# A PEER layer by dense matmuls over streamed expert tables in place of gathers

## The reference

```python
x = x + gate_m * y
h2 = rms_norm(x, norm_ffn) * (1 + scale_f) + shift_f
# for each token t, head h of 8
q = (h2 @ w_query).reshape(tokens, 8, 2, 128)
s = einsum('thpd,pkd->thpk', q, sub_keys)         # 2 x 128 key scores
s1, i1 = top_k(s[:, :, 0], 16); s2, i2 = top_k(s[:, :, 1], 16)
cand = s1[..., :, None] + s2[..., None, :]        # 256 sums
top_s, top_c = top_k(cand, 16)
e1, e2 = i1 at top_c // 16, i2 at top_c % 16
idx = e1 * 128 + e2                               # one of 16384 experts
g = softmax(top_s)
a = gelu(einsum('thkd,td->thk', expert_down[idx], h2))
out = x + gate_f * einsum('thk,thkd->td', g * a, expert_up[idx])
```

## Time and profile before

| | |
|---|---|
| median of 3 runs | 3375.26 us (3372.39 to 3380.6) |
| span of the profiled execution, first to last instruction | 3373.3 us |
| PE busy | 2396.1 us, 71% |
| DVE busy | 2288.6 us, 68% |
| ACT busy | 1584.8 us, 47% |
| POOL busy | 1313.6 us, 39% |
| DMA moved | 1143.75 MB, mean 339 GB/s |

### The profile page before, as it was taken

The page is one execution under the profiler, slowest core; times in us unless marked ns, Lnnn a source line. Parts: engine busy times, 40 slices in busy tenths (PEclk is TensorE's granted clock), DMA queues, the critical chain, the costliest instruction groups (busy, mean ns, idle before and its releaser), DMA issues.

```text
span 3373.3 us, 39537 instructions
## 1 busy us (share of the span) xinstructions
PE 2396.1 (71%) x13234; PEld 1954.9 (58%) x13234; DVE 2288.6 (68%) x6287; ACT 1584.8 (47%) x2643; POOL 1313.6 (39%) x1166
## 2 busy tenths in 40 slices
PE   5967899957666666766766667666666676666666
PEld 4654577526665555655565556555555566555555
DVE  6873665368987777767777767766777776775554
ACT  3213333215555555545555555555545554555454
POOL 1141600014544444444434444434444444444554
PEclk9989789978887767777777777777777777776666
DMA  6600100249999999999999999999999999999997
GB/s 240 183 13 16 51 1 1 102 176 416 420 421 414 421 408 422 409 421 409 421 401 421 407 421 409 421 408 420 403 421 406 421 408 421 409 421 414 419 421 324
DMA packets 172956, 1143.75 MB, mean 339 GB/s; under 512 B 22384, under 2 KB 23296, under 8 KB 41680
## 3 DMA queue, kind: packets, MB, share of 16 engines
q0 software_dynamic: 148352, 1077.61, 77.4%
q1 hardware_dynamic: 23168, 59.42, 4.9%
q10 hardware_dynamic: 1232, 4.20, 0.3%
HBM read 1131.59 MB, written 8.39 MB: 338 GB/s over the span
## 4 chain that ended last, share of the span: by engine, by line
DMA 42%; DVE 17%; PE 9%; issue 8%; ACT 5%; POOL 1%; POOLq 0%; DVEq 0%; SPq 0%
DMA pair_b<-in_experts_dram,idx_g 24%; DMA pair_a<-in_experts_dram,idx_g 17%; DVE pair_b L1480 4%; PE outs L1267 2%; DVE pair_a L1480 2%; PE outa L1267 2%; ACT pair_b L1348 2%; PE outs L1292 2%; PE outa L1292 2%; ACT pair_a L1348 2%; DMA wq<-in_w_query_dram 1%; DVE top_i L1405 1%; POOL pair_b L1224 1%; DVE top_i L1408 1%; DVE hot L1438 1%
## 5 line engine op out<-in xcount | busy, mean ns | idle before, releaser
L1224 POOL DMA_INDIRECT pair_b<-in_experts_dram,idx_g x612 | 714.1, 1167 | 835.9 <-PE outs L1267 382.4
L1480 DVE SCALAR_TENSOR_TENSOR pair_b<-pair_b,h 128x1024 f32<-128x1024 f32 x612 | 749.0, 1224 | 417.6 <-DMA pair_b<-in_experts_dram,idx_g 410.3
L1348 ACT ACTIVATE pair_b<-pair_b,w 128x1024 f32<-128x1024 f32 x612 | 697.1, 1139 | 306.2 <-DVE w L1474 299.6
L1224 POOL DMA_INDIRECT pair_a<-in_experts_dram,idx_g x412 | 479.8, 1165 | 718.4 <-PE outs L1267 273.6
L1480 DVE SCALAR_TENSOR_TENSOR pair_a<-pair_a,h 128x1024 f32<-128x1024 f32 x412 | 504.2, 1224 | 281.3 <-DMA pair_a<-in_experts_dram,idx_g 275.5
L1267 PE MATMUL outa<-ident,pair_b 128*128 128x128 f32 x2448 | 469.7, 358 | 239.9 <-ACT pair_b L1348 234.4
L1267 PE MATMUL outs<-ident,pair_b 128*128 128x128 f32 x2448 | 441.7, 343 | 246.8 <-ACT pair_b L1348 244.9
L1267 PEld LDWEIGHTS outa<-ident,pair_b 128*128 128x128 f32 x2448 | 384.9, 186 | 320.4 <-ACT pair_b L1348 315.6
L1348 ACT ACTIVATE pair_a<-pair_a,w 128x1024 f32<-128x1024 f32 x412 | 469.2, 1139 | 205.2 <-DVE w L1474 199.0
L1267 PEld LDWEIGHTS outs<-ident,pair_b 128*128 128x128 f32 x2448 | 363.4, 178 | 317.8 <-ACT pair_b L1348 317.6
L1344 ACT ACTIVATE ga<-a 128x1 f32<-128x1 f32 x1024 | 206.9, 202 | 697.9 <-DVE pair_b L1480 395.1
(11 more groups left out here) (343 smaller groups left out, 2508.1 us busy)
## 6 DMA issues: line engine op xcount, KB each, us to landing
wada<-in_w_ada_t_dram SPq DMA_DIRECT2D x48, 512.0 KB, 5.7
pair_b<-in_experts_dram,idx_g POOLq DMA_INDIRECT x612
wq<-in_w_query_dram SPq DMA_DIRECT2D x4, 2048.0 KB, 31.0
pair_a<-in_experts_dram,idx_g POOLq DMA_INDIRECT x412
ht<-in_x_t_dram ACTq DMA_DIRECT2D x4, 1024.0 KB, 16.1
wout<-in_w_out_dram SPq DMA_DIRECT2D x1, 4096.0 KB, 13.7
x<-in_x_dram SPq DMA_DIRECT2D x8, 512.0 KB, 6.5
out_dram<-x SPq DMA_DIRECT2D x8, 512.0 KB, 2.6
```

What stands on the lines that cost most here:

```text
L1224: p.indirect_dma_start(pair[n % R], None, A["experts"], bass.IndirectOffsetOnAxis(ap=idx[:, t % (2 * PH), k:k + 1], axis=0)).then_inc(pair ...
L1348: s_.activation(pair[n % R][:, D:], pair[n % R][:, D:], ACT.Copy, scale=w[:, n % NA:n % NA + 1]).then_inc(scaled, 1)
L1480: v.scalar_tensor_tensor(down, down, 1.0, S.h2[:, n // P, :], ALU.mult, ALU.mult, accum_out=a[:, n % NA:n % NA + 1]).then_inc(dotted, 1)
```

## The change

There are no gathers any more. All 16384 experts are computed for all tokens, and what a token did not pick is masked to zero.

- The tables are laid out anew outside of the launch: `down_units` and `up_units` are 128 units of 512 KB each. A unit is the 128 experts with one second key e2, over all first keys e1. SP streams them through a ring of six (`R = 6`).
- Tokens are four groups of 256, and each group has two passes, one for each half of the units. Phase A of a pass (`dots`) makes, for 64 units, dots of 128 experts with 256 tokens; ACT takes the gelu of two units at a time from PSUM into `dense`, 64 KB a partition. Phase B (`sums`) multiplies `dense` by the up units and accumulates in PSUM for the group. Phases A and B of different passes alternate: A0 A1 B0 A2 B1 A3 B2 and so on to B6 B7.
- The masks: for 8 tokens at a time DVE makes one-hot rows of e1 (`hot1`, 128 wide) and of e2 times the softmax weight (`hot2`, 64 wide) over the 128 picks of a token, PE multiplies the two for each token (`spread_gates`), and DVE multiplies `dense` by the outcome (`mask`). 32 such batches a pass are set between the units of the neighbouring phases, one after every two or three units.
- Queries and scores of all 64 tasks are done before the loop, a tile at a time after the next tile's output projection (`ask`). The scores (128 KB a task) and the transposed h2 go out to DRAM and come back by POOL's and SP's queues. The search is as before, 24 tasks before the loop over passes on DVE and 40 inside it; it keeps e1, e2 and the softmax weight (`picks`) instead of a joint index, and PE turns them (`turn_picks`).
- x2 is held two tiles at a time and spilled to the output in DRAM; the final sum is gated and added row by row (`finish`), with a fourth transposed row for the gate, so that the row transposes are 32 in place of 24.

```diff
-    R, NA = 10, 16
+    GROUP = 2 * P
+    GROUPS = SEQ // GROUP
+    HALF_E = PK // 2
+    PASSES = 2 * GROUPS
+    BT = 8
+    BATCHES = GROUP // BT
+    R = 6
...
+    phases = [("A", 0), ("A", 1)]
+    for p in range(PASSES - 2):
+        phases += [("B", p), ("A", p + 2)]
+    phases += [("B", PASSES - 2), ("B", PASSES - 1)]
...
         def _(sp):
...
+            for n in range(UNITS):
+                kind, p = phases[n // HALF_E]
+                u = n % HALF_E
...
+                if n >= R:
+                    sp.wait_ge(used, n - R + 1)
+                table = A["down_units"] if kind == "A" else A["up_units"]
+                sp.dma_start(ring[:, n % R], table[HALF_E * (p % 2) + u]).then_inc(unit_in[n % R], 16)
...
         def _(pool):
-            for n in range(SLOTS):
...
-                p.indirect_dma_start(pair[n % R], None, A["experts"],
-                                     bass.IndirectOffsetOnAxis(ap=idx[:, t % (2 * PH), k:k + 1], axis=0)).then_inc(pair_in[n % R], 16)
+            for task in range(TASKS):
+                pool.wait_ge(score_kept[task % 4], 16 * (task // 4 + 1))
+                if task >= 2:
+                    pool.wait_ge(s_read, task - 1)
+                pool.dma_start(tsc[:, task % 2], score_dram[task]).then_inc(tsc_in[task % 2], 16)
...
         def _(pe):
...
-            def add_up(n):
...
+            def ask(i):
+                turn(i)
+                for h in range(PH + 1):
+                    if h < PH:
+                        queries(PH * i + h)
+                    if h >= 1:
+                        scores(PH * i + h - 1)
...
+                else:
+                    ask(i - 1)
+            ask(NT - 1)
...
+            def spread_gates(p, b):
+                at = EVENT["gates", p, b]
+                pe.wait_ge(hot_ready, BATCHES * p + b + 1)
+                if at >= 2:
+                    pe.wait_ge(gate_read, at - 1)
+                for j in range(BT):
+                    last = t.matmul((qb, sb)[at % 2][:, j * HALF_E:(j + 1) * HALF_E], hot1[:, b % 2, j, :], hot2[:, b % 2, j, :],
+                                    start=True, stop=True)
+                last.then_inc(spread, 1)
+
+            def dots(n, p, u):
...
+                for k in range(KD):
+                    last = t.matmul(bank[:, (u % 2) * GROUP:(u % 2 + 1) * GROUP], ring[:, n % R, k * P:(k + 1) * P], hg[:, :, k, :],
+                                    start=k == 0, stop=k == KD - 1)
+                last.then_inc(used, 1)
+
+            def sums(n, p, u):
+                q = p // 2
+                if u == 0:
+                    pe.wait_ge(gate_read, EVENT["gates", p, BATCHES - 1] + 1)
...
+                for a in range(2):
+                    for half in range(2):
+                        last = t.matmul(accs[a][:, half * 512:(half + 1) * 512], bufs[p % 2][:, u, a * P:(a + 1) * P],
+                                        ring[:, n % R, half * 512:(half + 1) * 512],
+                                        start=p % 2 == 0 and u == 0, stop=p % 2 == 1 and u == HALF_E - 1)
+                last.then_inc(used, 1)
...
         def _(act):
...
+                    s_.activation(bufs[p % 2][:, 2 * m:2 * m + 2, :].rearrange("p u n -> p (u n)"), (t0, t1)[pair % 2][:],
+                                  ACT.Gelu_apprx_tanh).then_inc(gelu_done, 1)
+                    if p == 0 and m == 11:
+                        softened(1)
...
         def _(dve):
...
+            def make_hot(p, b):
...
+                own.mark(v.tensor_tensor(hot2[:, b % 2], bcast(iota_f[:, half * HALF_E:(half + 1) * HALF_E], 1, [P, BT, HALF_E]),
+                                         bcast(e2, 2, [P, BT, HALF_E]), ALU.is_equal))
+                own.step(v.tensor_tensor(hot1[:, b % 2], bcast(iota_f[:], 1, [P, BT, PK]), bcast(e1, 2, [P, BT, PK]), ALU.is_equal))
+                v.tensor_tensor(hot2[:, b % 2], hot2[:, b % 2], bcast(g, 2, [P, BT, HALF_E]), ALU.mult).then_inc(hot_ready, 1)
+
+            def mask(p, b):
...
+                v.tensor_tensor(dense, (qb, sb)[at % 2][:].rearrange("p (t e) -> p e t", t=BT), dense, ALU.mult).then_inc(gate_read, 1)
...
+            for p in range(PASSES):
+                make_hot(p, 0)
+                for b in range(BATCHES):
+                    if b + 1 < BATCHES:
+                        make_hot(p, b + 1)
+                    mask(p, b)
+                    if 1 <= p <= NT - 3:
+                        task = PH * (p + 2) + b // 4
+                        for m in ((0, 1), (2,), (3, 4), (5,))[b % 4]:
+                            find_part(task, m)
```

More of the change, by code:

```diff
@@ L1115, in phase_f @@
[L1115 to L1136, removed]
@@ new lines, in phase_f @@
+    for p in range(PASSES):
+        for b in range(BATCHES):
+            order.append(("gates", p, b))
+            if p == 0 and b == 20:
+                order.append(("picks", 2))
+        if 1 <= p <= NT - 3:
+            order.append(("picks", p + 2))
+    EVENT = {event: n for n, event in enumerate(order)}
+    wq = place(nc, "wq", [P, PH // 2, KD, 4 * PK], 0)
+    bufs = [place(nc, f"dense{n}", [P, HALF_E, GROUP], at) for n, at in enumerate((0, 103))]
+    x2 = place(nc, "x2", [P, 2, D], 64)
@@ new lines, in phase_f @@
+    cand = place(nc, "cand", [P, 2, TOPK, TOPK], 96)
+    hot = place(nc, "hot", [P, 2, TOPK, TOPK], 98)
+    s2 = place(nc, "s2", [P, 2, PK], 100)
+    tsc = place(nc, "task_scores", [P, 2, 2 * PK], 101)
+    part = place(nc, "part", [P, 2, D], 135)
+    h2t = place(nc, "h2t", [P, 2, KD, P], 143)
+    ring = place(nc, "units", [P, R, D], 167)
+    picks_t = place(nc, "picks_t", [P, 2, 2, 3, P], 192)
+    wout = S.wout
+    row_cols = (S.mod[:, GATE_M:GATE_M + KD], S.a_f[:], S.mod[:, SHIFT_F:SHIFT_F + KD], S.mod[:, GATE_F:GATE_F + KD])
@@ L1199, in _ @@
[L1199 to L1205, removed]
+                sp.dma_start(out[i], x2[:, i % 2]).then_inc(spilled, 16)
+                if i + 2 < NT:
+                    sp.wait_ge(spilled, 16 * (i + 1))
+                    sp.wait_ge(std2_ready, i + 1)
+                    sp.wait_ge(h2_ready, i + 1)
+                    sp.dma_start(x2[:, i % 2], x[i + 2]).then_inc(x_in[i % 2], 16)
@@ L1206, in _ @@
+            store(GROUPS - 1)
             sp.wait_ge(stored, 16 * NT)
@@ L1284, in _ @@
                 last.then_inc(rows_done, 1)
[L1285 removed]
+            pe.wait_ge(rows_out, 8)
             for i in range(NT):
@@ L1310, in _, with turn_picks @@
             pe.wait_ge(a_out, NT)
             pe.wait_ge(b_read, NT)
-            for n in range(SLOTS):
-                if n in TURNED:
-                    turn(TURNED[n])
-                if n in ASKED:
-                    queries(ASKED[n])
-                if n in SCORED:
-                    scores(SCORED[n])
-                if n % P == 12 and n > P:
-                    turn_back(n // P - 1)
-                add_up(n)
-            turn_back(NT - 1)
+            def turn_picks(i):
+                at = EVENT["picks", i]
+                pe.wait_ge(picks_ready, i + 1)
+                if at >= 2:
+                    pe.wait_ge(gate_read, at - 1)
+                for n in range(3):
+                    last = t.transpose((qb, sb)[at % 2][:, n * P:(n + 1) * P], picks[i % 2][:, n, :], S.ident[:])
+                last.then_inc(spread, 1)
@@ new lines, in softened, with answered @@
+            def softened(i):
+                act.wait_ge(less_ready, i + 1)
+                s_.activation(picks[i % 2][:, 2, :], picks[i % 2][:, 2, :], ACT.Exp).then_inc(exp_ready, 1)
+            def answered(i):
+                turned(i)
+                for h in range(PH + 1):
+                    if h < PH:
+                        queried(PH * i + h)
+                    if h >= 1:
+                        scored(PH * i + h - 1)
+                    if i == NT - 2 and h == 4:
+                        square(NT - 1)
@@ L1544, in _ @@
-            finish(NT - 1)
-            close(NT - 1)
+                    own.step(v.scalar_tensor_tensor(pt, x2[:, j % 2], rs[:, 2, j:j + 1], rows[1], ALU.mult, ALU.mult))
+                    v.tensor_tensor(pt, pt, rows[2], ALU.add).then_inc(h2_ready, 1)
+                if i >= 2:
+                    find(2 * (i - 2))
+                    find(2 * (i - 2) + 1)
+                if i == 5:
+                    weigh_less(0)
+                elif i == 7:
+                    weigh(0)
+            find(14)
```

450 lines of the change are left out of this document (244 added, 206 removed).

## The result

The kernel now takes half as long again: 5063.7 us (median of 4 runs, 5061.6 to 5068.7) against 3375.1 us (median of 4 runs, 3372.4 to 3380.6), a ratio of 1.500 with an interval of 1.498 to 1.502. The forecast was 5054 us. The profiled execution took 5063.6 us, with a span of 5061.5 us.

A forecast was written before the change was run, and what follows sets the result against it. TensorE was to replace bytes as the bound: 1061 us before the loop, 3981.5 of TensorE work, 2 of hand-overs and 8 at the end make a 5052 us span; 2 added gives 5054 us, range 4995 to 5210.

The forecast's parts named there:

- first output matmul: Start of the last phase's first output matmul: 603.72 us before, plus 1.2 for eight more row transposes, 604.9 us.
- from there to the loop: From the first output matmul to the loop: 374.4 us of TensorE work, 61.4 of stalls, 20 of low clock.
- gates and all that their groups cost: `spread_gates` in the loop: 2048 matmuls of 64 columns, 4096 records at 107 ns, 438.3 us.
- hand-overs: In the loop, B0 and B7 wait for the last mask right before them, 1 us each, 2 us.
- the straight line through 128 and 512 columns: Record price by column count, 0.828 ns a column; gave 217.5 ns for the 256-column records of `dots`.
- The stage before the loop: Output projections, queries and scores of all tiles before the loop over passes; was to end at 1061 us.
- the clock's price: Before the loop: slower query records after a TensorE stall, 2.5 us for each of 8 stalls, 20 us.
- The covers: Beside TensorE's loop: VectorE batches of 5.6 to 6.0 us, ScalarE's gelu and 135 GB/s of loads all stay hidden.
- Rival 2: Before the loop: scores through DRAM late for the search, or `wq` late for `ask(0)`; 50 to 150 us more; chance 0.12.
- Rival 3: In the loop, VectorE's gate chain paces TensorE once a batch takes over 12.1 us; 5440 us; chance 0.08.
- Rival 4: TensorE's clock does not hold in the loop: 6760 us at 0.7, or 5500 to 5700; chance 0.05.
- Rival 5: Expert matmuls take one record, not two, total 3065 us; or sustained streams compress, total 3660 us; chance 0.02.

The follow-up runs named there:

- The experiment that asks later: Against the changed kernel: a third `part` buffer, and after each output projection the queries of tile i-2 in place of i-1; 4994.5 us.

## Why the prediction was right

**What bounds it.** The prediction moved the bound from bytes to TensorE and charged every record in full. Both are shown: 3986.1 of 3988.0 us busy, and 111.6 ns back for each gate record left out.

**The terms.** Predicted and measured, on the span (where the whole loop has no break, a term is its count times its measured record):

| term | predicted | measured | off by |
|---|---|---|---|
| first output matmul | 604.9 | 606.9 | +2.0 |
| from there to the loop | 455.8 | 458.4 | +2.6 |
| `dots` | 1781.8 | 1768 (8192 x 215.8) | -14 |
| `sums` | 1758.8 | 1759 (4096 x 429.4) | 0 |
| gates and all that their groups cost | 438.3 | 457.4 | +19 |
| `turn_picks`, hand-overs | 4.6 | 4.2 (2.6 as predicted, 1.6) | 0 |
| end | 8 | 8.0 (5053.5 to 5061.5) | 0 |
| span | 5052 | 5061.5 | +9.5 |

The gates' 457.4 us are what is left of the loop's 3988.2 (1065.3 to 5053.5) when the other terms are taken off, 111.7 ns a record. The timeline splits them: 4096 x 108.1 = 443 us for the records themselves, against 438 predicted, and 14 to 15 us for entering and leaving the groups, which stretches the records of `dots` between them from 215.8 to 217.5 ns. That last cost the sum did not have. (The kernel with 2 gate records a group shows that the other 14 cost 111.6 ns each.) Against it, the straight line through 128 and 512 columns set the pure `dots` record 1.7 ns too high; the lower bound, half a 512-column record (214.7 ns), was nearer. The two errors nearly cancel, so that the span came out to 10 us is in part luck.

**The stage before the loop** was right to 3 us, by sizes that were each a little off. It began 2.0 us late: the phases ahead of it, which the change doesn't touch, handed over at 601.05 in this execution and at 598.19 in the one before, 2.9 us later, and the eight more row transposes cost 0.4 us where 1.2 were set down. The wait for VectorE was 6.6 us seven times, where the earlier trace rows gave 6.4; the clock's price was 3.2 us each time (1.1 on the `turn`, 2.1 on the queries) in place of 2.5. The experiment that asks later took 67.5 us back, 9.6 us a round, at the place where the stall was put. One thing stays open. `ask(7)` found its tile ready, as the prediction said, and still took 9.04 us for its first queries, at a granted clock of 0.81; in five of the other kernels they took 9.04 us too. The kernel that asks later has the same two gaps ahead of its last two tiles, and there the queries took 7.41 us at 1.00. TensorE's timeline for the last tile, in the changed kernel and in that one:

```profile
1028.09 1.06 PE L1286 MATMUL pgg<-ident,part 128*128 128x128 f32 x8 [0.67 <-ACT staged L1447]
1030.33 9.04 PE L1299 MATMUL pgg<-h2t,wq 128*128 128x128 f32 x64 [1.17 <-ACT h2t L1433]
```

```profile
960.53 1.06 PE L1286 MATMUL pgg<-ident,part 128*128 128x128 f32 x8 [0.67 <-ACT staged L1448]
962.77 7.41 PE L1299 MATMUL pgg<-h2t,wq 128*128 128x128 f32 x64 [1.18 <-ACT h2t L1434]
```

So the gaps alone do not account for that lower clock.

**The covers.** A batch of VectorE costs less than predicted, since the strided mask took 0.69 us and not up to 1.09 (the earlier trace rows was no guide to it). The load of a unit landed in 3.2 us where 5.7 was taken from the earlier trace rows:

```profile
units<-in_down_units_dram SPq DMA_DIRECT2D x512, 512.0 KB, 3.2
...
wq<-in_w_query_dram SPq DMA_DIRECT2D x4, 2048.0 KB, 17.6
```

**The rivals.** Rival 2: `wq` landed in 17.6 us and TensorE did not wait for it; VectorE waited for no scores. Rival 3: no wait for `hot`, and none for a mask but the two hand-overs of 0.8 us; with VectorE loaded to beyond the threshold the wait for `hot` appears, and with it the lower clock. Rival 4: the clock was 1.00 over the loop. The Trainium skill ("TensorE: Matmul & The Clock Gate", Part 1) says that one or two busy cores never trip its limiter; the trace of this one core agrees. Rival 5: two records for each float32 matmul in all three kinds, and streams of thousands of records showed no shorter spacing than the groups of 16 in the earlier trace rows. The 131 ns that the Trainium skill ("TensorE: Matmul & The Clock Gate", Back-to-back issue gap) gives for 512 columns in sustained streams is not seen in bfloat16 either, where eight records in a row stand at 216 ns each, that section's figure for a single one.

## What to carry to other kernels

Before trading gathers for dense work, price the dense work in TensorE records by start-to-start times of series that the trace already has: here 3986 us of matmuls stand where gathers set some 2590 us, and the operand type of the dense products (float32 at four times the price of bfloat16) decided the sign. That compares rounded products with unrounded gathers; rounding the gathers' tables too was not tried. A per-token mask product in float32 costs its stationary tile, with 64 columns as with 8. When an engine waits for an answer to something it has only just given the input for, put one more tile between the two: here the wait went, and with it the low clock behind it.

## What was not expected of the hardware

- A 6.6 us wait of TensorE cost 3.2 us more in slower work behind it; a 1.1 us wait alone cost almost nothing (7.41 us for 64 query records, where 7.14 is unbroken). Two gaps of 0.7 and 1.2 us close together came before first queries of 9.04 us at a granted clock of 0.81 in the changed kernel, and before first queries of 7.41 us at 1.00, twice, in the one that asks later.
- A group of 16 gate records set between 256-column records costs some 0.06 us beyond its own 1.73 us (8.69 us in all, with 6.91 for 32 unbroken records of `dots`).
- VectorE's product of a bfloat16 one-hot and a float32 broadcast weight, written as bfloat16, took 692 ns at 512 elements, the same as all in float32.
- In the loop a bfloat16 stationary tile loads in 101 to 110 ns (group means), a float32 one in 190 to 192 ns.
